# The opening of a streaming encoder step: the norm's row of weights moves into the operand splits

## The reference

```python
def rms_norm(x, g):
    return x * lax.rsqrt(jnp.mean(x * x, axis=-1, keepdims=True) + EPS) * g

h = rms_norm(x, ln_mix_g)
u, vg, q, k, v, gates = split(h @ w_in)                # the input projection
a_out = gmlp_spatial(gelu(u), layer_norm(gelu(vg)), w_s, b_s)
b_out = windowed attention with sinks over q, k, v and the cache
x = x + (sigmoid(g_A) * (a_out @ w_pa) + sigmoid(g_B) * (b_out @ w_pb)) @ w_o
x = x + (gelu(conv3(h2 @ w_up_gate)) * (h2 @ w_up_val)) @ w_down,  h2 = rms_norm(x, ln_ffn_g)
y = rms_norm(x, ln_final_g)
```

## Time and profile before

| what | us |
|---|---|
| median of 3 runs | 1638.52 |
| lowest and highest | 1637.5, 1639.94 |
| span of the profiled execution | 1639.4 |
| TensorE busy in it | 1613.6 (98%) |
| VectorE busy | 1144.4 (70%) |
| ScalarE busy | 710.3 (43%) |
| GpSimd busy | 75.9 (5%) |

### The profile page before, as it was taken

The page is one execution under the profiler, slowest core; times in us unless marked ns, Lnnn a source line. Parts: engine busy times, 40 slices in busy tenths (PEclk is TensorE's granted clock), DMA queues, the critical chain, the costliest instruction groups (busy, mean ns, idle before and its releaser), DMA issues. The chain is left out here.

```text
span 1639.4 us, 32455 instructions
## 1 busy us (share of the span) xinstructions
PE 1613.6 (98%) x12887; PEld 1574.8 (96%) x12887; DVE 1144.4 (70%) x2076; ACT 710.3 (43%) x1308; POOL 75.9 (5%) x145
## 2 busy tenths in 40 slices
PE   7999999999999999999999999999999999999998
PEld 7999999999999999999999999999999999999997
DVE  7666565656658868786625888888888776757566
ACT  7344445444444336364434543333443345434312
POOL 1000000000000000001112100000000000100001
PEclk9999999999999999999999999999999999999999
DMA  9354434343437864757743233333233227566322
GB/s 291 111 157 122 123 112 133 101 139 101 120 108 204 242 210 172 242 163 167 163 144 104 59 107 107 107 107 102 97 98 104 80 80 268 130 197 183 98 76 111
DMA packets 272490, 227.05 MB, mean 138 GB/s; under 512 B 43343, under 2 KB 223379, under 8 KB 272339
## 3 DMA queue, kind: packets, MB, share of 16 engines
q1 hardware_dynamic: 137662, 149.90, 27.7%
q10 hardware_dynamic: 131285, 66.16, 14.5%
q0 software_dynamic: 3392, 8.91, 3.2%
HBM read 150.56 MB, written 74.36 MB: 137 GB/s over the span
## 5 line engine op out<-in xcount | busy, mean ns | idle before, releaser
L2354 PE MATMUL ps<-op_hi,w_hi 128*128 128x272 f32 x3672 | 775.9, 292 | 8.8 <-DVE w_lo L1655 4.0
L2354 PE MATMUL ps<-op_hi,w_lo 128*128 128x272 f32 x3672 | 760.8, 289 | 0.0
L2354 PE MATMUL ps<-op_lo,w_hi 128*128 128x272 f32 x3672 | 759.0, 288 | 0.0
L2354 PEld LDWEIGHTS ps<-op_hi,w_hi 128*128 128x128 f32 x3672 | 576.4, 189 | 25.7 <-issue 20.2
L2354 PEld LDWEIGHTS ps<-op_lo,w_hi 128*128 128x128 f32 x3672 | 578.6, 189 | 0.0
L2354 PEld LDWEIGHTS ps<-op_hi,w_lo 128*128 128x128 f32 x3672 | 575.2, 189 | 0.0
L1655 DVE TENSOR_TENSOR w_lo<-raw,w_hi 128x512 fp32r<-128x512 f32 x256 | 173.8, 698 | 163.5 <-ACT w_hi L1229 163.4
L1229 ACT ACTIVATE w_hi<-raw 128x512 fp32r<-128x512 f32 x256 | 153.6, 625 | 131.7 <-PE ps L2354 81.8
L1303 ACT ACTIVATE u<-ps 128x544 f32<-128x544 f32 x106 | 66.1, 624 | 228.0 <-PE ps L2354 227.8
L1229 ACT ACTIVATE w_hi<-w_f 128x512 fp32r<-128x512 f32 x159 | 95.8, 626 | 43.7 <-DVE w_f L1675 25.0
L1655 DVE TENSOR_TENSOR w_lo<-w_f,w_hi 128x512 fp32r<-128x512 f32 x159 | 104.8, 683 | 5.3 <-ACT w_hi L1229 4.6
(11 more groups left out here) (200 smaller groups left out, 1507.4 us busy)
## 6 DMA issues: line engine op xcount, KB each, us to landing
in_spill<-quad SPq DMA_DIRECT2D x88, 272.0 KB, 2.2
raw<-in_w_up_dram ACTq DMA_DIRECT2D x44, 512.0 KB, 5.1
raw<-in_w_in_dram ACTq DMA_DIRECT2D x42, 512.0 KB, 5.3
g_spill<-value_out SPq DMA_DIRECT2D x22, 544.0 KB, 2.7
t_spill<-t_buf SPq DMA_DIRECT2D x8, 1088.0 KB, 4.3
lo_f<-g_spill SPq DMA_DIRECT2D x8, 1088.0 KB, 5.6
lo_f<-t_spill SPq DMA_DIRECT2D x8, 1088.0 KB, 7.5
raw<-in_w_down_dram ACTq DMA_DIRECT2D x16, 512.0 KB, 5.1
```

Of the source, the lines that this page charges most:

```text
L2354: last = pe.matmul(out[:, h, 0:HB], (w_hi, w_lo)[a][place][:, j, :], (op_hi, op_lo)[b][at][:, j, HB * h:HB * h + HB], start=fresh and j == ...
```

## The change

- The norm of a tile no longer multiplies by `mix_g`. It is two operations of 4 x 128 with the spread rstd read once for all four (L1667). The blocks hold x times rstd.
- `mix_g` comes in at the splits: the copies of `op_hi` 0, 1, 7, 6 take a column of it as scale, the subtractions of `op_lo` become `scalar_tensor_tensor`.
- The block sums `t_sum` become four operations each, with `mix_g` or its negative (`minus_g`) as the scalar. `hi_f[3]` is scaled in place by four more ScalarE operations (`gain_b11`) once its low parts are made. `t_sum` 1 goes ahead of `t3_sum`, which now is `lo_f[5]` minus `hi_f[3]`. `op_hi` 3, which overwrites `hi_f[3]`, waits for it (`s_t3`).
- VectorE copies tiles 0, 2 and 6, ScalarE the others (`DVE_COPIES`).
- Tile 5 is turned inside pair 0, and the places of the other transposes and spreads move (`beside_first`). TensorE does 12 transposes of the identity at the start and 10 ahead of the first product, which nobody reads (`keep_warm`).
- Seven small loads (`tab_rows`) move from the head of ScalarE's queue to SP, behind the stores of tiles 0 to 3. The load of pair 1's weights moves on ScalarE from the fourth quarter of slot 0 to the third of slot 3. The semaphore `s_r2`, wanted much later, is folded into `s_rb_p`.

```diff
-COPIED = tuple(range(1, NT)) + ("tables",)
-
-NORMED = ("gains", "copy") + tuple((n, 0, k) for n in range(SPLIT + 1) for k in range(2)) \
-    + tuple((n, 1, k) for n in range(SPLIT, NT) for k in range(2))
+DVE_COPIES = (0, 2, 6)
+COPIED = tuple(n for n in range(NT) if n not in DVE_COPIES) + ("tables",)
+
+NORMED = ("gains", ("copy", 0), (0, 0, 0), (0, 0, 1), ("copy", 2)) + tuple((n, 0, k) for n in range(1, SPLIT + 1) for k in range(2)) \
+    + tuple((n, 1, k) for n in (SPLIT, SPLIT + 1) for k in range(2)) + (("copy", 6),) \
+    + tuple((n, 1, k) for n in range(SPLIT + 2, NT) for k in range(2))
+
+GAINED = {0: 0, 1: 1, 7: 0, 6: 1}
...
+        def copied_tile(engine, n):
+
+            if n in DVE_COPIES:
+                engine.wait_ge(s_hf, NORMED.index(("copy", n)) + 1)
+            else:
+                engine.wait_ge(s_xts, COPIED.index(n) + 1)
...
+            for n in range(4):
+                store_xt(n)
+            sp.dma_start(tab_rows[FT + KT:FT + 2 * KT, 1, :], ln_mix_g[0].rearrange("(f p) -> f p", p=P)).then_inc(s_tab_in, 16)
...
             sp.dma_start(ws_raw[:], w_s[0].rearrange("g t s -> t g s")).then_inc(s_par_in, 16)
-            for n in range(NT):
+            for n in range(4, NT):
                 store_xt(n)
...
-            act.dma_start(tab_rows[FT + KT:FT + 2 * KT, 1, :], ln_mix_g[0].rearrange("(f p) -> f p", p=P)).then_inc(s_tab_in, 16)
...
                 if g == 0 and n == 3:
                     act.wait_ge(s_op, op_count(0, 0))
-                act.activation(op_hi[at][:, j], operand_source(g, n)[:, j], copy).then_inc(s_op_hi, 1)
+                    act.wait_ge(s_t3, 1)
+                if g == 0 and n in GAINED:
+                    kt = 2 * int(part) + GAINED[n]
+                    act.activation(op_hi[at][:, j], operand_source(g, n)[:, j], copy, scale=mix_g[:, kt:kt + 1]).then_inc(s_op_hi, 1)
+                else:
+                    act.activation(op_hi[at][:, j], operand_source(g, n)[:, j], copy).then_inc(s_op_hi, 1)
...
+            def gain_b11(k):
+
+                act.wait_ge(s_op, op_count(0, 0, str(k)))
+                act.activation(hi_f[3][:, k], hi_f[3][:, k], copy, scale=mix_g[:, 2 * k:2 * k + 1]).then_inc(s_b11, 1)
+
             square_x(0)
             for n in range(1, SPLIT + 1):
                 square_x(n)
-                x_tile(n)
+                if n in COPIED:
+                    x_tile(n)
             weight_hi(0, 0)
             weight_hi(0, 4)
-            square_x(5)
             for k in range(KP):
                 operand_hi(0, 0, str(k))
+            square_x(5)
             x_tile(5)
...
                 if j == 0 and k in (3, 4):
                     for i in range(KP):
                         operand_hi(0, {3: 7, 4: 6}[k], str(i))
+                    if k == 4:
+                        for i in range(KP):
+                            gain_b11(i)
                 if (k, j) == (6, 2):
...
-                        if (k, j) == ((1, 2) if not plain(p) and plain(p - 1) and p > 2 else (0, 3)) and p + 1 < NPAIR:
+                        if (k, j) == ((1, 2) if not plain(p) and plain(p - 1) and p > 2 else (3, 2) if p == 0 else (0, 3)) and p + 1 < NPAIR:
                             load_weights(act, p + 1)
...
             def gains():
                 dve.wait_ge(s_tab_p, 1)
+                dve.tensor_scalar(minus_g, reg[2][:, 1, P:P + KT].rearrange("p (i k) -> p k i", k=2)[:, 1], -1.0, None, ALU.mult)
                 dve.tensor_copy(mix_g, reg[2][:, 1, P:P + KT]).then_inc(s_hf, 1)
 
-            def first_copy():
-                dve.wait_ge(s_xt_p, 1)
-                dve.tensor_copy(xts[0][:], turned_at[0].rearrange("p b (k t) -> p (b k) t", k=4)).then_inc(s_hf, 1)
+            def copy_tile(n):
+                dve.wait_ge(s_xt_p, n + 1)
+                dve.tensor_copy(xts[n][:], turned_at[n].rearrange("p b (k t) -> p (b k) t", k=4)).then_inc(s_hf, 1)
 
             def x_tile(n, half):
 
-                if n:
-                    dve.wait_ge(s_xts, COPIED.index(n) + 1)
-                else:
-                    dve.wait_ge(s_hf, NORMED.index("copy") + 1)
+                copied_tile(dve, n)
                 dve.wait_ge(s_rb_p, n + 1)
                 a, b = max(0, half * QT - n * P), min(rows_of(n), (half + 1) * QT - n * P)
                 t0 = n * P + a - half * QT
                 for k in range(2):
-                    for i in range(KP):
-                        kt = 2 * i + k
-                        last = dve.scalar_tensor_tensor(place_of(half, k)[:, i, t0:t0 + b - a], xts[n][:, kt, a:b], mix_g[:, kt:kt + 1],
-                                                        side[:, n % 2, a:b], ALU.mult, ALU.mult)
-                    last.then_inc(s_hf, 1)
+                    dve.tensor_tensor(place_of(half, k)[:, :, t0:t0 + b - a], xts[n].rearrange("p (i k) t -> p k i t", k=2)[:, k, :, a:b],
+                                      side[:, n % 2, a:b].unsqueeze(1).broadcast_to([P, KP, b - a]), ALU.mult).then_inc(s_hf, 1)
...
+                if g == 0 and n in GAINED:
+                    kt = 2 * int(part) + GAINED[n]
+                    dve.scalar_tensor_tensor(op_lo[at][:, j], operand_source(g, n)[:, j], mix_g[:, kt:kt + 1], op_hi[at][:, j].bitcast(F32),
+                                             ALU.mult, ALU.subtract).then_inc(s_op, 1)
+                else:
+                    dve.tensor_tensor(op_lo[at][:, j], operand_source(g, n)[:, j], op_hi[at][:, j].bitcast(F32), ALU.subtract).then_inc(s_op, 1)
...
-                    if i == 0:
-                        dve.tensor_tensor(lo_f[3][:], lo_f[4][:], hi_f[3][:], ALU.subtract).then_inc(s_t, 1)
-                    if i == 1:
-                        dve.wait_ge(s_t, 1)
-                        dve.tensor_tensor(lo_f[5][:], hi_f[4][:], lo_f[3][:], ALU.subtract).then_inc(s_t, 1)
+                    dve.wait_ge(s_b11, KP)
+                    if i:
+                        dve.wait_ge(s_t, i)
                     if i == 2:
-
-                        dve.wait_ge(s_t, 2)
-                        dve.wait_ge(s_t3, 1)
                         dve.wait_ge(s_op, op_count(0, 6))
-                        dve.tensor_tensor(hi_f[4][:], lo_f[5][:], hi_f[5][:], ALU.subtract).then_inc(s_t, 1)
+                    for k in range(KP):
+                        even, odd, minus = (mix_g[:, 2 * k:2 * k + 1], mix_g[:, 2 * k + 1:2 * k + 2], minus_g[:, k:k + 1])
+                        if i == 0:
+                            last = dve.scalar_tensor_tensor(lo_f[3][:, k], lo_f[4][:, k], even, hi_f[3][:, k], ALU.mult, ALU.subtract)
+                        if i == 1:
+                            last = dve.scalar_tensor_tensor(lo_f[5][:, k], hi_f[4][:, k], odd, lo_f[3][:, k], ALU.mult, ALU.subtract)
+                        if i == 2:
+                            last = dve.scalar_tensor_tensor(hi_f[4][:, k], hi_f[5][:, k], minus, lo_f[5][:, k], ALU.mult, ALU.add)
+                    last.then_inc(s_t, 1)
...
             def t3_sum(g):
 
                 dve.wait_ge(s_op, op_count(g, 7))
-                dve.wait_ge(s_t, t_count(g, 0))
+                dve.wait_ge(s_t, t_count(g, 0 if g else 1))
                 if g == 0:
-                    dve.tensor_tensor(lo_f[4][:], hi_f[4][:], lo_f[4][:], ALU.subtract).then_inc(s_t3, 1)
...
             gains()
-            first_copy()
-            for n in range(SPLIT + 1):
+            copy_tile(0)
+            x_tile(0, 0)
+            copy_tile(2)
+            for n in range(1, SPLIT + 1):
                 x_tile(n, 0)
             weight_lo(0, 0)
             for k in range(KP):
@@ -1752,13 +1781,17 @@
             weight_lo(0, 1)
             for k in range(KP):
                 operand_lo(0, 1, str(k))
+            for n in (SPLIT, SPLIT + 1):
+                x_tile(n, 1)
             weight_lo(0, 5)
-            for n in range(SPLIT, NT):
+            copy_tile(6)
+            for n in range(SPLIT + 2, NT):
                 x_tile(n, 1)
             for n in (7, 6):
                 for k in range(KP):
                     operand_lo(0, n, str(k))
             t_sum(0, 0, "w")
+            t_sum(0, 1, "w")
             t3_sum(0)
...
-                            sums = {(5, 0): ((1, "w"),), (6, 3): ((2, "w"),)}
+                            sums = {(6, 3): ((2, "w"),)}
...
-                if n == 3:
-                    pe.wait_ge(s_hf, NORMED.index("copy") + 1)
-                if n > 3:
-                    pe.wait_ge(s_xts, COPIED.index(n - 3 if n < 6 else n - 1) + 1)
+                if n > 2:
+                    copied_tile(pe, n - 3 if n < 6 else n - 1)
...
+            def keep_warm(count):
+                for _ in range(count):
+                    pe.transpose(reg[2][:, 0, 0:P], ident[:], ident[:])
+
+            keep_warm(12)
             pe.wait_ge(s_gain_in, 16)
             pe.transpose(reg[2][:, 1, P:P + KT], gain_rows[:], ident[0:KT, 0:KT]).then_inc(s_tab_p, 1)
-            for n in range(6):
+            for n in range(SPLIT + 1):
```

(11 more changed lines are left out.)

33 lines of the change are left out of this document (15 added, 18 removed).

## The result

| kernel | median us | lowest, highest | runs | against before |
|---|---|---|---|---|
| before | 1638.72 | 1637.5, 1639.94 | 4 | |
| changed | 1645.84 | 1643.83, 1646.24 | 4 | 1.0037 [1.0026, 1.0049] |

The change makes the kernel slower by 0.37%, 7.1 us between the medians; 1645.2 was predicted, +6.7. Beside the earlier trace rows, TensorE is busy for 3.7 us more, with the 22 fillers in it, on a span of 1644.1.

The account below looks back on a forecast made before the run. TensorE, busy 98% of the span, was taken as the bound, so only its stands and low clock count: +5.8 us at the transposes of V plus 0.9 for the first stand's clock gave +6.7, 1645.2 us, range 1641.0 to 1648.5.

Parts of the forecast that it names:

- The opening: Ahead of the first product: it starts at about 16.6, 2.9 us earlier, with the clock kept for 2.4 us more.
- The stand for tile 6: Inside pair 0: TensorE stands 2.9 us, from 25.2 to 28.1, for VectorE's copy of tile 6 before turning tile 7.
- The clock behind it: After the tile 6 stand: a possible clock fall costing between nothing and 2.4 us, taken as 0.9.
- `op_hi` 7: Late in pair 0: ScalarE starts splitting operand 7 at 35.15, against 36.57 before.
- Scalings and sums: Behind op_hi 7: scalings 2.6 us, two sums of 2.85 and t3_sum 2.4, ending at 52.1 against 47.46 before.
- The wait for `s_t3` and the copy of Q12: Ahead of pair 1: Q12's copy queues behind t3_sum, TensorE stands 6.5 us, pair 1 starts at 55.7, not 50.7.
- The clock behind the second stand: At the start of pair 1: the clock is low after the 6.5 us stand, costing 2.4 us.
- bias2 just in time: Ahead of the transposes of V: bias2 is ready by 77.7, before TensorE needs it at 78.9.
- The sum at V: At the first transposes of V: 78.9 against 73.07, 5.8 us later, plus 0.9 for the first stand's clock: +6.7.
- Rival (a): At both TensorE stands: the clock falls each time, +8 to +9 us, 1647; chance 0.30.
- Rival (c): At pair 1: the opening's gain carries through, ScalarE's s_t3 wait never coming last, 1637.0 to 1635.4; chance 0.05.
- the twelve fillers: At the start: they save up to 1.5 us on tiles 0 and 1 or nothing; the sum stays the same.

Follow-up runs that it names:

- e1: Changed kernel with ScalarE's split of op_hi 3 moved behind the copy of Q12 and pair 1's weights; 1644.21 us, ratio 1.0037 to before.
- e2: Changed kernel with op_hi 3 later on ScalarE and pair 1's low weights ahead of and between VectorE's block sums; 1639.58 us, 0.9998 to before.
- e7: Changed kernel without the twelve fillers at the very start; 1647.67 us, ratio 1.0048 to before.
- e10: Changed kernel with the seven small tables and the load of pair 1's weights put back in their old places; 1647.12 us, ratio 1.0044 to before.
- e4: Changed kernel with the edits of e2 and e3 together; 1637.20 us, ratio 0.9989 to before.
- e6: Changed kernel without the ten fillers just ahead of the first product; 1647.92 us, ratio 1.0054 to before.
- e8: Changed kernel without the four gain_b11 scalings, a part of the computation left out; 1645.38 us, ratio 1.0029 to before.
- e3: Changed kernel with tile 6 copied by ScalarE again, as before; 1642.39 us, ratio 1.0020 to before.
- e12: e5 without the ten fillers ahead of the first product; 1637.66 us, ratio 0.9988 to before.
- e5: e4 with three VectorE steps moved: first block sum, memset of ws_t and the bias2 operations go earlier; 1633.98 us, ratio 0.9961 to before.
- e11: Kernel before with 26 fillers ahead of the first product and the bias2 operations ahead of pair 2's first weight sum; 1634.06 us, ratio 0.9960.
- e9: Kernel before with only 26 fillers added ahead of the first product, behind a wait for tile 4's copy; 1636.81 us, ratio 0.9983.

## Why the prediction was right, step by step

- **The opening**: first product forecast at 16.6 at full clock; 16.40 at full clock. The idle stretch ahead of it forecast at about 1.5, measured 1.76. The norm's operation of 512 takes 679 ns, forecast 0.68.
- **The stand for tile 6**: from 25.2 to 28.1, 2.9 us; it ended at 28.14 after 2.77.
- **The clock behind it**: taken at 0.9 between 0 and 2.4. It fell in the profiled execution and cost 1.56: from the start of tile 7 to the product behind the second quadrant 11.01 us, where e1, whose clock stayed, took 9.45 (27.73 to 37.18). In e1, e2 and e7 the same stand cost no clock.
- **`op_hi` 7**: forecast 35.15, measured 37.48. Of the 2.3 us 1.56 are the clock, which the sum held as a lump; 0.8 were undercounted in the quarters, spreads and norms between. By then nothing of the opening's gain was left: `op_hi` 7 started 0.9 us later than before, where the forecast had it 1.4 earlier.
- **Scalings and sums**: from `op_hi` 7 to the end of `t3_sum` forecast 16.95 us, measured 17.22. Two errors nearly cancel in this: the 0.5 for the load of weights was nothing (e10), and from the start of the first sum to the end of `t3_sum` it took 8.82 us where 8.1 was forecast, 0.54 of it a wait of VectorE between the two sums that the forecast did not have. With a pointer a VectorE piece of 544 takes 780 ns (forecast 0.78), a ScalarE one 742 (forecast 744).
- **The wait for `s_t3` and the copy of Q12**: forecast 3.5 us from the start of `op_hi` 3 to the start of pair 1, and 3.50 measured. The stand forecast 6.5, measured 6.42. Pair 1 started at 58.32 instead of 55.7; the difference is the two items above. e1 showed what the prediction had not said: even with Q12 copied in time, the low weights behind the sums would have held TensorE 3.5 us. The chain had two ends.
- **The clock behind the second stand**: forecast 2.4; half clock until 62.8, and from 58.32 to V 22.73 us against 20.8 without: 1.93.
- **bias2 just in time**: forecast 77.7 against 78.9; measured 80.85 against 81.05. With 0.2 us between them, bias2 alone would have held V at 80.85 had the clock stayed; e1, where V waits for bias2, shows it.
- **The sum at V**: +6.7 with the 0.9 counted in, measured +7.98; at the end +7.1 between medians. The miss at V, 1.3 us, is 0.7 for the clock, 0.8 for the undercount, 0.3 for the sums and 0.5 less for the second fall.

Rival (a), the clock lost at both stands, is what the profiled execution did: +7.98 at V, where it had +8 to +9. Since e1, e2 and e7 kept the clock at the first stand, the median of 1645.84 may be a mix of the two, between the forecast and its 1647; which of the four runs did which isn't known, and the profiled run itself, with both falls, took 1645.92. So the mechanism is shown and the number is in part luck: the 0.9 us was a guess between two outcomes, errors of 0.3 to 0.8 us of both signs stand in the other terms, and the 7.98 us at V became 7.1 between the medians. Rival (c), the gain carried through, needed `t3_sum` to end by 45.7; it ended 9 us later, and e4 showed that even without the stands bias2 takes most of the gain at V. The prediction set the span of 1639.4 beside the median of 1638.52 as if both were times of a run; by the 1.8 us above, that execution took about 2.7 us more than the median. The sum, which adds +6.7 to the median, doesn't hang on it. The term of the forecast that was furthest off is the chain from tile 7 to `op_hi` 7, clock included; two items priced at nothing or by guess were also off, the twelve fillers (some tenths) and the load of weights (nothing instead of 0.5).

## What to carry to other kernels

A wait that is added where an engine overwrites a buffer is paid by everything queued behind it on that engine; look there for the copy that frees another engine, and let it go first. Work taken off the opening is only worth what the next wait that ends last leaves of it: here bias2 had to move before either the rewritten norm or the 26 idle transposes showed more than 1 us at V. And before an opening is rewritten for speed, price its clock: the fillers with one moved step alone were worth 0.4%, all that the rewrite reached in its best order.

## What the runs showed of the hardware

**After the same short gap the clock fell in some executions and not in others.** The same stand of 2.77 to 2.78 us ahead of tile 7 was followed by half clock in four of seven profiles (the change, e6, e8, e10) and not in three (e1, e2, e7). The windows of the change above and this one of e1 show the two, and the slow stretches lasted from 3 to over 6 us:

```profile
28.00:32.00 4.00, 4.00 (x37) 3.78 (x36) 1.28 (x2) 2.11 (x4) 0.73 (x2) 1.00 1.13 337
```

A gap of 1.27 us within pair 0, which has the same length in all eleven kernels built on the change, was followed by half clock in four (e3, e8, e10, e12), as here in e3 behind the gap that ended at 35.12:

```profile
36.00:38.00 2.00, 2.00 (x11) 2.00 (x10) 1.81 (x4) 2.00 (x5) 0.00 (x0) 0.50 0.81 225
39.00:41.00 2.00, 2.00 (x18) 2.00 (x18) 1.17 (x2) 2.00 (x4) 0.00 (x0) 1.00 1.19 316
```

Ahead of the first product none of the gaps of up to 1.76 us was, and each of 2.40 us or more (before, e6, e12) was. The Trainium skill (TensorE: Matmul & The Clock Gate, HAM oscillation — how this bites in real kernels) tells of a loop in which TensorE waits some 3 to 5 us for a load in each round, and the clock falls in every one. For the shorter stands of 2.8 us here the runs differ: four of seven. How much of the scatter of single runs comes from this is not shown: e1 (1641.4 to 1648.3 in eight) and e12 (1635.4 to 1643.8 in twelve) scatter widely and e5 and e11 little (1.6 and 2.5 us in five each), but the change and e7, which have the stand of 2.8 us, scatter little too (2.4 in four, 2.7 in five). What decides within one length of gap, no run here shows.

**The first transposes went faster behind idle ones.** The first 16 transposes of x took 3.59 us (before) and 3.68 (e7, e9, e11) with no fillers ahead, and 2.22 to 3.43 in ten profiles behind twelve, though the granted clock reads 1.00 in both.
